# A chunked delta-rule scan: triangle inverses built from 32x32 blocks, with the last level joining them

## What is computed

```python
def rwkv7_step(S, inp):
    r, w, k, v, kk, kka = inp
    sa = jnp.einsum('dbhij,dbhj->dbhi', S, -kk)
    S = S * w[..., None, :] + sa[..., :, None] * kka[..., None, :] + v[..., :, None] * k[..., None, :]
    y = jnp.einsum('dbhij,dbhj->dbhi', S, r)
    return S, y
...
    S0 = jnp.zeros((N_DIR, B, RWKV_HEADS, HEAD_DIM, HEAD_DIM), jnp.float32)
    _, ys = lax.scan(rwkv7_step, S0, xs)
    ys = ys.transpose(1, 2, 0, 3, 4)
    y = ys[0] + jnp.flip(ys[1], axis=1)
```

## Time and profile before

| what | value |
|---|---|
| median of three executions | 3638.68 us |
| profiled execution, its own time | 3639.07 us |
| its span, first to last instruction | 3637.3 us |
| granted TensorE clock, mean | 0.983 of full speed |
| TensorE busy (matrix multiplications) | 3478.2 us, 96% of the span |
| VectorE busy | 1954.3 us, 54% |
| ScalarE busy | 1253.4 us, 34% |
| scan, from its first multiplication to its last | 2797.6 to about 3046.6 us |

### The profile page before, as it was taken

How to read it: one execution, slowest core, us unless ns; L and a number is a source line. 1 busy time by engine, 2 the same in 40 slices (tenths; PEclk the granted TensorE clock), 3 DMA queues, 4 the chain that set the end, 5 groups by cost and what they waited for, 6 DMA issues and landing times.

```text
span 3637.3 us, 56212 instructions
## 1 busy us (share of the span) xinstructions
PE 3478.2 (96%) x23343; PEld 2871.5 (79%) x23343; DVE 1954.3 (54%) x2685; ACT 1253.4 (34%) x1598; POOL 0.2 (0%) x4
## 2 busy tenths in 40 slices
PE   9999999998999999999999989999999887999998
PEld 7778888887788877778887768887887875888887
DVE  4565736436574653565344355344676666845434
ACT  3474424324342441443223343223532113333222
POOL 0000000000000000000000000000000000000000
PEclk9999999999999999999999999999999999999999
DMA  4102232221123222113222212222233002022231
GB/s 155 58 1 93 93 103 93 93 98 42 58 93 104 93 95 98 41 58 104 93 99 98 81 58 93 93 96 101 91 108 137 4 5 91 5 81 93 93 104 70
DMA packets 50432, 297.10 MB, mean 82 GB/s; under 512 B 6848, under 2 KB 7872, under 8 KB 17349
## 3 DMA queue, kind: packets, MB, share of 16 engines
q1 hardware_dynamic: 39376, 269.92, 21.9%
q10 hardware_dynamic: 10868, 24.41, 1.8%
HBM read 283.99 MB, written 10.33 MB: 81 GB/s over the span
## 4 chain that ended last, share of the span: by engine, by line
PE 90%; DVE 7%; ACT 2%; issue 1%; DMA 0%; DVEq 0%; ACTq 0%; PEldq 0%
PE PS L334 13%; PE PS L336 13%; PE PS L335 13%; PE PS L449 8%; PE PS L450 7%; PE PS L451 7%; PE PS L1902 2%; PE PS L1903 2%; PE PS L1904 2%; PE PS L2409 1%; PE PS L1219 1%; PE PS L2826 1%; PE PS L2412 1%; PE PS L1199 1%; PE PS L215 1%
## 5 line engine op out<-in xcount | busy, mean ns | idle before, releaser
L171 DVE TENSOR_TENSOR WL<-W,WH 128x2048 fp32r<-128x2048 f32 x254 | 582.1, 2292 | 729.3 <-ACT WH L161 723.6
L161 ACT ACTIVATE WH<-W 128x2048 fp32r<-128x2048 f32 x254 | 485.8, 1912 | 1105.2 <-PE PS L451 578.0
L334 PE MATMUL PS<-XH,WH 128*128 128x512 f32 x2144 | 837.8, 391 | 4.3 <-issue 4.3
L335 PE MATMUL PS<-XL,WH 128*128 128x512 f32 x2144 | 835.1, 390 | 0.0
L336 PE MATMUL PS<-XH,WL 128*128 128x512 f32 x2144 | 835.0, 389 | 0.0
L334 PEld LDWEIGHTS PS<-XH,WH 128*128 128x128 f32 x2144 | 403.1, 188 | 93.7 <-issue 10.6
L335 PEld LDWEIGHTS PS<-XL,WH 128*128 128x128 f32 x2144 | 403.1, 188 | 84.5 <-issue 1.0
L336 PEld LDWEIGHTS PS<-XH,WL 128*128 128x128 f32 x2144 | 403.0, 188 | 84.0
L689 DVE TENSOR_TENSOR PS<-PS,R 128x512 f32<-128x512 f32 x248 | 170.9, 696 | 442.4 <-PE PS L336 439.8
L449 PE MATMUL PS<-HH,WH 128*128 128x512 f32 (+1 forms) x960 | 374.7, 390 | 1.2
L451 PE MATMUL PS<-HH,WL 128*128 128x512 f32 (+1 forms) x960 | 373.6, 389 | 0.0
(11 more groups left out here) (480 smaller groups left out, 4607.9 us busy)
## 6 DMA issues: line engine op xcount, KB each, us to landing
W<-in_weights SPq DMA_DIRECT2D x254, 1024.0 KB, 4.9
gate_spill<-slots ACTq DMA_DIRECT2D x16, 256.0 KB, 2.1
gates<-gate_spill ACTq DMA_DIRECT2D x2, 2048.0 KB
x_spill<-X ACTq DMA_DIRECT2D x1, 2048.0 KB, 8.0
X<-x_spill ACTq DMA_DIRECT2D x1, 2048.0 KB
out<-X ACTq DMA_DIRECT2D x8, 256.0 KB, 2.1
W<-in_weights SPq DMA_DIRECT2D x2, 512.0 KB, 5.0
X<-in_x ACTq DMA_DIRECT2D x4, 256.0 KB, 7.2
```

The lines of the kernel that those rows point to most:

```text
L161: P.e.activation(K.WH[:, s, :], K.W[:, s, :], ACT.Copy).then_inc(P.sem("hi_ready"), P.adds("hi_ready"))
L171: P.e.tensor_tensor(K.WL[:, s, :], K.W[:, s, :], K.WH[:, s, :].bitcast(F32), ALU.subtract).then_inc(P.sem("weights_split"), P.adds("weight ...
L334: P.e.matmul(out, wh[:, k, c], xh[:, k, r], start=(k == 0), stop=False)
L335: P.e.matmul(out, wh[:, k, c], xl[:, k, r], start=False, stop=False)
```

## The change

The levels below 64 now work on 32x32 blocks in tiles of half the width, and the last level (b = 32) writes only the block that joins two 32x32 inverses:

- The 64x64 tiles `c_n`, `c_p`, `c_y` (4 x 64 columns) become `b_n`, `b_p`, `b_y` (4 x 32 columns) and hold the two diagonal 32x32 blocks of each 64x64 matrix; the partitions stay 128. The masks shrink from 1024 to 544 columns.
- TensorE's `grams` takes the place of the first `fill`: it writes the diagonal blocks of both kinds (64 multiplications of 32 columns for a full chunk) and the block off the diagonal, `b_across` (16 more).
- `below` and `doubled` issue one multiplication for each 32x32 block: 16 and 32 for each direction and level where there were 8 and 16.
- The last level is `joined`: 8 multiplications for each direction, a copy, 8 for each direction, and VectorE copies the joining block into `c_pf` (two copies for each direction on 32 partitions).
- The two additions of VectorE's `doubled` become one over both halves of `b_p`, and so do the two additions of the identity. `begin` has one more copy (`b_across`).
- ScalarE copies the diagonal blocks from `b_p` into `c_pf` with four operations of 32 partitions, after the last doubling level (`inverse_ready`, due 10, or 4 for the meta chunk). Two waits on that (`diagonal_ready`) are new: TensorE ahead of `solution`, VectorE ahead of the next `begin`.
- VectorE clears `c_pf` once, in the meta chunk.

```diff
+        def grams(c, freed):
+
+            for name in freed:
+                P.e.wait_ge(P.sem(name), P.due(name))
+            for kind, at in (("ab", 0), ("ba", 256)):
+                for d, F, t, q, cols in each(c):
+                    left, right = (src(c, d, x, F, q) for x in kind)
+                    for j in range(2):
+                        b = slice(32 * j, 32 * j + 32)
+                        last = mm(K.PS[t.start + 32 * j:t.start + 32 * j + 32, 6 + d, at + 32 * q:at + 32 * q + 32], left[:, b], right[:, b], start=True, stop=True)
+            if c >= 0:
+                for d, F, t, q, cols in each(c):
+                    a, b = 1 - d, d
+                    last = mm(K.PS[t.start + 32 * a:t.start + 32 * a + 32, 6 + d, 128 + 32 * q:160 + 32 * q],
+                              src(c, d, "a", F, q)[:, 32 * a:32 * a + 32], src(c, d, "b", F, q)[:, 32 * b:32 * b + 32], start=True, stop=True)
...
         def below(n):
 
             for d in range(self.dirs(n)):
                 P.e.wait_ge(P.sem("inverse_ready"), P.due("inverse_ready"))
-                for F, t, q, at in one_way(n, d):
-                    last = mm(K.PS[t, d, at:at + 64], K.c_n[t, d, q, :], K.c_p[t, 0, d, q, :], start=True, stop=True)
+                for q in range(4):
+                    for rows in self.BLOCKS32:
+                        last = mm(K.PS[rows, d, 32 * q:32 * q + 32], K.b_n[rows, d, q, :], K.b_p[rows, 0, d, q, :], start=True, stop=True)
...
-        def doubled(n, final=False):
+        def doubled(n):
+
             for d in range(self.dirs(n)):
                 P.e.wait_ge(P.sem("below_ready"), P.due("below_ready"))
-                for F, t, q, at in one_way(n, d):
-                    last = mm(K.PS[t, d, at:at + 64], K.c_p[t, 1, d, q, :], K.c_y[t, d, q, :], start=True, stop=True)
-                if not final:
-                    for F, t, q, at in one_way(n, d):
-                        last = mm(K.PS[t, d, 256 + at:320 + at], K.c_y[t, d, q, :], K.c_p[t, 1, d, q, :], start=True, stop=True)
+                for q in range(4):
+                    for rows in self.BLOCKS32:
+                        last = mm(K.PS[rows, d, 32 * q:32 * q + 32], K.b_p[rows, 1, d, q, :], K.b_y[rows, d, q, :], start=True, stop=True)
+                for q in range(4):
+                    for rows in self.BLOCKS32:
+                        last = mm(K.PS[rows, d, 128 + 32 * q:160 + 32 * q], K.b_y[rows, d, q, :], K.b_p[rows, 1, d, q, :], start=True, stop=True)
+                last.then_inc(P.sem("inverse_done"), P.adds("inverse_done"))
+
+        def joined():
+
+            for d in range(2):
+                P.e.wait_ge(P.sem("inverse_ready"), P.due("inverse_ready"))
+                for q in range(4):
+                    for a, b in self.across(d):
+                        last = mm(K.PS[b:b + 32, d, 32 * q:32 * q + 32], K.b_across[a:a + 32, d, q, :], K.b_p[a:a + 32, 0, d, q, :], start=True, stop=True)
+                last.then_inc(P.sem("below_done"), P.adds("below_done"))
...
+                P.e.wait_ge(P.sem("inverse_ready"), P.due("inverse_ready", 10 if n >= 0 else 4))
+                for j, rows in enumerate(self.BLOCKS32):
+                    last = P.e.activation(K.c_pf[rows, 0:m, :, 32 * (j % 2):32 * (j % 2) + 32], K.b_p[rows, 0, 0:m, :, :], ACT.Copy)
+                last.then_inc(P.sem("diagonal_ready"), P.adds("diagonal_ready"))
...
+            P.e.wait_ge(P.sem("diagonal_ready"), P.due("diagonal_ready"))
             P.e.wait_ge(P.sem("rhs_ready"), P.due("rhs_ready"))
```

More of the change, by code:

```diff
@@ L2279, in one, with across, small @@
         return K.PS[:, bank, :].rearrange("p (d q n) -> p d q n", d=2, q=4)[:, 0:n]
+    BLOCKS32 = [slice(32 * j, 32 * j + 32) for j in range(4)]
+    def across(self, d):
+        return [(64 * t + 32 * (1 - d), 64 * t + 32 * d) for t in range(2)]
+    def small(self, K, bank, at, n):
+        return K.PS[:, bank:bank + n, at:at + 128].rearrange("p d (q n) -> p d q n", q=4)
     def two(self, K, bank, half, n):
@@ new lines, in doubled @@
+                for q in range(4):
[9 more added lines that the diff above has]
+                last.then_inc(P.sem("below_done"), P.adds("below_done"))
+            for d in range(2):
+                P.e.wait_ge(P.sem("below_ready"), P.due("below_ready"))
+                for q in range(4):
+                    for a, b in self.across(d):
+                        last = mm(K.PS[b:b + 32, d, 32 * q:32 * q + 32], K.b_p[b:b + 32, 1, d, q, :], K.b_y[b:b + 32, d, q, :], start=True, stop=True)
@@ L2418, in pe @@
             if n is not None:
-                fill(("N", "ab"), n, ("rows_ready",) if full else ())
+                grams(n, ("rows_ready",) if full else ())
             elif c is not None:
@@ L2441, in pe @@
             below(n)
-            doubled(n, not full)
+            doubled(n)
             fill(("v_rows",), n, ("rows_ready",))
@@ L2515, in dve @@
             full, m = n >= 0, self.dirs(n)
-            begin(m)
+            begin(m, full)
             below(m, 0)
@@ L2530, in dve @@
                 masked(K.c_rb, self.two(K, 6, 0, m), K.c_incl[:, 0:m, :], m)
-            masked(K.c_ak, self.two(K, 6, 1 if full else 0, m), K.c_strict[:, 1:1 + m, :], m).then_inc(P.sem("grams_masked"), P.adds("grams_masked"))
+            masked(K.c_ak, self.two(K, 6, 1 if full else 0, m), K.c_strict[:, 0:m, :], m).then_inc(P.sem("grams_masked"), P.adds("grams_masked"))
             below(m, 1)
@@ L2537, in dve @@
             below(m, 2)
-            doubled(m, not full)
+            doubled(m)
             if full:
@@ L3002, in level @@
         return (row // (2 * b) == col // (2 * b)) & (lo // b % 2 == 0) & (hi // b % 2 == 1)
-    masks = [strict[d] for d in (1, 0, 1)] + [level(d, 1) for d in (1, 0, 1)] + [level(d, b) for b in (2, 4, 8, 16, 32) for d in range(2)]
-    more = [strict[d] | (row == col) for d in range(2)] + [row == col]
+    more = [strict[d] | (row == col) for d in range(2)] + [(r % 32)[:, None] == np.arange(32)[None, :]]
+    masks = [strict[d] for d in range(2)]
+    row, col = (r % 32)[:, None], np.arange(32)[None, :]
+    masks += [row > col, row < col] + [level(d, 1) for d in (1, 0, 1)] + [level(d, b) for b in (2, 4, 8, 16) for d in range(2)]
     head = (r[:, None] // 64) == (r[None, :] // 64)
@@ L3223, in program @@
             quad = lambda name: (name, [128, 2, 4, 64])
-            K.c_n, K.c_p, K.c_pf, K.c_y, K.c_r, K.c_u = row(ha, rest, quad("c_n"), ("c_p", [128, 2, 2, 4, 64]), quad("c_pf"), quad("c_y"), quad("c_r"), quad("c_u"))
+            blocks = lambda name: (name, [128, 2, 4, 32])
+            K.b_n, K.b_across, K.b_p, K.b_y, K.c_pf, K.c_r, K.c_u = row(ha, rest, blocks("b_n"), blocks("b_across"), ("b_p", [128, 2, 2, 4, 32]), blocks("b_y"), quad("c_pf"), quad("c_r"), quad("c_u"))
             K.c_bT, K.c_kT, K.c_ak = row(None, rest + 80, *(quad(n) for n in ("c_bT", "c_kT", "c_ak")))
```

75 lines of the change are left out of this document (43 added, 32 removed).

## The result

The changed kernel takes **3740.51 us** (median of four runs, 3738.17 to 3743.39) against 3638.03 for the kernel before, run beside it: a ratio of 1.0281 [1.0263, 1.0299], +102.5 us. The forecast was 3755.4, in a range of 3725 to 3785. The profiled execution took 3742.81 us, its span is 3741.0 us, 103.7 more than before.

A forecast was written before the change was run, and what follows sets the result against it. The prediction took the supply of TensorE's instruction blocks, 3.74 us each, as the bound in the eight full steps. 105.3 + 8 x (0.4 + 0.6) + 3 = 116.3 us on 3639.1 gave 3755.4 us, range 3725 to 3785.

The forecast's parts named there:

- The loop of instruction blocks: In the eight full steps, TensorE waits for each 16 KB block of 256 instructions, 3.74 us per block.
- More multiplications: In the eight full steps, 240 more multiplications each make 58.5 blocks 88.5: +105.3 us.
- The join: The last level of each full step lasts about 4.1 us against 3.74: +0.4 us per step, between 0 and 1.
- the clock: In the full steps, TensorE may fall to 1.2 GHz in places: 0.6 us per step, between 0 and 2.7.
- The meta chunk: Its 96 calls more, 1.5 blocks, cost between 0 and 5.6 us, taken as 3.
- Shorter multiplications: In the levels, 16 calls in four tiles take at best 0.23 us; the gain was booked at nothing.
- VectorE and ScalarE's copies: In the full steps, VectorE's fewer, no longer operations and ScalarE's four copies during the join were taken at nothing.
- The first: Rival for the full steps: multiplications are the bound, the even distance is chance; 27 us faster, 3612 us; chance 0.04.
- The second: Rival: the clock falls to 1.2 GHz for most of the scan; +17, about 3772 us; chance 0.12.
- The third: Rival: in the full steps, changes of tile size drain the array; 9 us, 3765 us; chance 0.08.
- The fourth: Rival for the full steps: blocks come faster, at 3.3 us each, or two at once; 3710 us; chance 0.06.

The follow-up runs named there:

- e8: The kernel before with two more 128x256 VectorE operations ahead of each y of the levels: 3667.3 us, ratio 1.0077 to the kernel before.
- e6: The kernel before with c_n, c_p and c_y held in bf16, with less precision in the levels: 3591.5 us, ratio 0.9873 to the kernel before.
- e7: The changed kernel with two more 128x128 VectorE operations ahead of each y of the levels: 3742.1 us, ratio 1.0293 to the kernel before.
- e5: The changed kernel with its small blocks held in bf16, all calls kept: 3641.4 us, ratio 1.0015 to the kernel before.
- e3: The kernel before with Gram products merged in pairs, 448 calls per step for 480, those with k later: 3625.0 us, ratio 0.9967.
- e9: The kernel before with 240 unneeded calls more per full step, 32x4 weights and 4 moved columns: 3748.6 us, ratio 1.0306.
- e4: The changed kernel without half of the small calls and with c_r multiplied by zero: 3643.9 us, ratio 1.0016 to the kernel before.
- e1: The kernel before with 240 unneeded calls more per full step, 64x64 weights and 4 moved columns: 3798.0 us, ratio 1.0451.

## Why the prediction was right

**The bound.** The loop of instruction blocks is what the forecast stood on, and it held: 89 packets (182 in the whole execution, for the forecast 181), 22656 records, a first step of 37.6 us and seven of 40.6 to 42.6, "issue" as first cause at even intervals, TensorE busy for 70% of the stretch. The kernel before was nearer to its next bound than "218.8 of the 225.7 us are this loop" lets one think. By e8 the chain through VectorE had some 30 us of room in the eight steps (55.4 - 25.4), by e6 about 42 (225.7 - 183.5): estimates, about 4 to 5 us per step. It made no difference to the sum, since the change lengthened one side only. And "issue" is 14.9 us there over all lines, not only the 4.5 of the largest.

**More multiplications**, 88.5 x 3.74 - 225.7 = +105.3: measured +101.8. The 3.70 us are the stretch divided by its blocks and so hold all that is in it. The starts of the 89 packets say the same without that division: 3.68 us apart on average, from 3.34 to 4.52, half of them at 3.60 or less. The main term was 3.5 us too high.

**The small terms were mis-sized.** *The join* and *the clock* were to cost 8 us together. The eight packet intervals in which most of a join lies average 3.66 us, those with nothing of it 3.68; the 4.02 us between two stops above are one case. The 47 intervals that lie wholly at a clock of 0.50 average 3.70 us, the 11 at full clock 3.66: over all 88 that is under 4 us (an estimate). *The meta chunk* was to cost 3 us; its stretch is 16.9 us for 17.0, and the full steps start 0.3 us later. So the small terms gave 10.7 us too much and the block 3.5; 1.6 us more behind the stretch came in, and the profiled execution grew by 103.7 where 116.3 stood. The median lies 2.3 us below the profiled execution. These are differences of single executions, and the four of the changed kernel spread over 5.2 us, so terms of one or two us can't be told from nothing. I added three prices to a bound that hides what is shorter than itself, after having booked the shorter multiplications at nothing for just that reason.

**Shorter multiplications, VectorE and ScalarE's copies at nothing.** Right: e7 for VectorE; the copies end before TensorE's last products of the join. The calls are as short as said, two groups of 16 at the full clock:

```profile
2864.59 0.45 PE L2442 MATMUL PS<-b_y,b_p 32*32 32x32 f32 x32
...
2864.86 0.45 PE L2445 MATMUL PS<-b_p,b_y 32*32 32x32 f32 x30
```

32 records, 16 calls, in 0.45 us, and the second group beside the first, starting 0.27 us later.

**The rivals.** The first (faster) needed a block in under 2.5 us; it has 3.70. The rule of the Trainium skill ("Runtime: NRT & Kernel Launch", "Instruction fetch mechanics"), by which the crossing is mostly hidden, doesn't hold for this stretch. The second (the clock) had its condition right and its price wrong: the clock stood at 0.50 for some 70% of the stretch, which a mean of 0.65 gives, not "in places". Its price rested on 7.9 us for the 224 calls of a step, which the earlier trace rows don't give: 14 groups of sixteen at 0.47 us are 6.6 us, 13.2 at half the clock, and that is no more than the 13.1 us of their 3.5 blocks. Two stretches:

```profile
2833.90:2861.20 27.30, 20.59 (x924) 18.80 (x927) 7.47 (x22) 3.71 (x8) 0.00 (x0) 0.50 0.02 5
2861.20:2874.90 13.70, 8.68 (x574) 7.89 (x570) 5.25 (x12) 1.48 (x4) 0.00 (x0) 1.00 0.01 4
```

Blocks are as long at either clock (above), and TensorE still stands for 30% of the stretch (99 of 327.5 us). I read this as the lower clock filling part of what would else be standing still. The third (tile changes) would have given 3765 and isn't in the total; e5 has the same changes at +5.5 us. What one costs by itself was not measured. The fourth, blocks at 3.3 us, was not seen as a mean: 3.70 (e5: 3.69). Single intervals get down to it: 3.34 us after, and 3.35 before, below the 3.48 that the prediction took for the shortest. The low end of its range, at 3.5 us for each block, was a mean that no run shows.

## What to carry to other kernels

Where a kernel's code runs straight through once, as here, count TensorE's instructions. Stops put down to "issue" at an even distance, each followed by an instruction packet, meant here that the count sets the time and not the size of the calls; adding calls of little work is the test for it. Then fewer, wider calls pay (e3, 0.3%), and smaller tiles cost (here 3.7 us for each 64 fp32 calls). And a cost shorter than the bound that hides it isn't added on top of it.

## What the runs showed that I had not expected

- A clock of 0.50 in 70% of the scan cost next to nothing: blocks took 3.70 us there and 3.66 at full clock. e9, with the same 88.5 blocks and other calls, had 0.87 and took 338.8 us for the 327.5 of the changed kernel.
- The price of a block hardly depends on what is in it: 3.69 us (e5, bf16), 3.70 (the changed kernel), 3.74 (e7), 3.77 (e4), 3.83 (e9), as long as nothing else sets the time.
- A call with 4 moved columns isn't cheap if its weights are 64x64: 32 ns a record at full clock, and 240 of them per step made the array the bound for much of the stretch (e1, 4.35 us per block); 32x4 weights took 11 ns a record (e9).
- A product of bf16 takes half the instructions of one in fp32, and the levels in bf16 gain 1.3% (e6), with 14 blocks fewer.
